# The head of a hybrid decoder step computed by halves of the channels

## What is computed

```python
def rmsnorm(x, g):
    xf = x.astype(jnp.float32)
    y = xf * lax.rsqrt(jnp.mean(xf * xf, axis=-1, keepdims=True) + EPS)
    return y.astype(x.dtype) * g

def modulate(x, g, shift, scale):
    return rmsnorm(x, g) * (1 + scale[:, None, :]) + shift[:, None, :]
...
        mod = (jax.nn.silu(c) @ ada_w[i] + ada_b[i]).reshape(c.shape[0], N_MOD, D_MODEL)
        hn = modulate(x, norm_g[i, 0], mod[:, 0], mod[:, 1])
...
            out, C1, n1, m1 = mlstm_mixer(hn, C0s[j], n0s[j], m0s[j], mlstm_w_in[j],
                                          mlstm_b_gates[j], mlstm_head_g[j], mlstm_w_out[j])
```

## Time and profile before

| what | us |
|---|---|
| median of 3 runs | 1310.14 |
| lowest and highest | 1308.98 and 1311.0 |
| the profiled execution's own time | 1309.41 |
| its span | 1307.7 |
| PE busy | 1269.4 |
| ScalarE, VectorE, GpSimd busy | 504.7, 772.1, 367.6 |

### The profile page before, as it was taken

One profiled execution on the slowest core, in us unless ns is written; L12 is line 12 of the kernel. 1 busy time (PEld: TensorE's weight loads), 2 busy tenths in 40 slices (PEclk: granted clock), 3 DMA queues, 4 the chain that ended last, 5 costly groups with the idle time before them and its releaser, 6 DMA issues.

```text
span 1307.7 us, 26354 instructions
## 1 busy us (share of the span) xinstructions
PE 1269.4 (97%) x11305; PEld 1243.4 (95%) x11305; DVE 772.1 (59%) x1296; ACT 504.7 (39%) x792; POOL 367.6 (28%) x184
## 2 busy tenths in 40 slices
PE   5799999999999999999999999999999999999996
PEld 4799999999999999999999999999999999999996
DVE  2623445667757643643659809859859743824764
ACT  3533453222532551551552322123362551642721
POOL 2434433443300041041044245435310041050050
PEclk9999999999999999999999999999999999999998
DMA  9667214754456574574553233323132242342321
GB/s 332 204 193 177 80 55 122 230 169 123 135 173 195 161 229 126 162 228 128 160 165 97 65 97 92 86 83 97 53 94 81 68 134 60 97 132 62 98 65 69
DMA packets 242526, 169.34 MB, mean 129 GB/s; under 512 B 5851, under 2 KB 217055, under 8 KB 242282
## 3 DMA queue, kind: packets, MB, share of 16 engines
q1 hardware_dynamic: 215946, 121.33, 32.4%
q10 hardware_dynamic: 26304, 46.27, 10.9%
q0 software_dynamic: 160, 0.07, 0.0%
HBM read 160.70 MB, written 6.94 MB: 128 GB/s over the span
## 4 chain that ended last, share of the span: by engine, by line
PE 80%; DVE 10%; issue 3%; DMA 3%; SPq 2%; ACT 2%; POOL 1%; POOLq 0%; DVEq 0%; ACTq 0%
PE G L1922 39%; PE G L2042 19%; PE G L1948 9%; PE G L2078 6%; PE B L2106 3%; SPq L462 1%; DVE hb L1396 1%; DMA raw<-in_mlp_w_down 1%; DVE small_s L1847 1%; DVE acc L1273 1%; DMA early<-in_ada_w 1%; PE B L1908 1%; DVE yc L1846 1%; DVE Xl L1410 1%; PE B L2290 1%
## 5 line engine op out<-in xcount | busy, mean ns | idle before, releaser
L1087 POOL TENSOR_TENSOR wl<-raw,wh 128x1024 fp32r<-128x1024 f32 x128 | 326.4, 2558 | 784.1 <-ACT wh L587 781.2
L587 ACT ACTIVATE wh<-raw 128x1024 fp32r<-128x1024 f32 x144 | 152.1, 1056 | 277.0 <-PE G L1922 147.4
L1922 PE MATMUL G<-Hh,wh 128*128 128x272 f32 x864 | 179.3, 289 | 0.0
L1922 PE MATMUL G<-Hh,wl 128*128 128x272 f32 x864 | 178.4, 288 | 0.0
L1922 PE MATMUL G<-Hl,wh 128*128 128x272 f32 x864 | 178.3, 288 | 0.0
L1922 PE MATMUL G<-Xh,wh 128*128 128x272 f32 x672 | 143.1, 294 | 1.0 <-POOL wl L1087 1.0
L1922 PE MATMUL G<-Xl,wh 128*128 128x272 f32 x672 | 138.7, 288 | 0.0
L1922 PE MATMUL G<-Xh,wl 128*128 128x272 f32 x672 | 138.3, 287 | 0.0
L1922 PEld LDWEIGHTS G<-Hh,wh 128*128 128x128 f32 x864 | 135.5, 188 | 1.0 <-issue 1.0
L1922 PEld LDWEIGHTS G<-Hl,wh 128*128 128x128 f32 x864 | 135.8, 189 | 0.0
L1922 PEld LDWEIGHTS G<-Hh,wl 128*128 128x128 f32 x864 | 135.0, 189 | 0.0
(11 more groups left out here) (385 smaller groups left out, 2732.0 us busy)
## 6 DMA issues: line engine op xcount, KB each, us to landing
raw<-in_mlp_w_up SPq DMA_DIRECT2D x64, 512.0 KB, 4.2
raw<-in_mlp_w_down SPq DMA_DIRECT2D x64, 512.0 KB, 4.4
aring<-in_ada_w ACTq DMA_DIRECT2D x60, 512.0 KB, 5.1
raw<-in_mlstm_w_in SPq DMA_DIRECT2D x24, 512.0 KB, 4.3
raw<-in_conv_w_in SPq DMA_DIRECT2D x24, 512.0 KB, 3.7
early<-in_ada_w SPq DMA_DIRECT2D x16, 512.0 KB, 12.2
free_l<-in_ada_w ACTq DMA_DIRECT2D x20, 256.0 KB, 6.8
raw<-in_mlstm_w_out SPq DMA_DIRECT2D x8, 512.0 KB, 4.7
```

Of the source, the lines that this page charges most:

```text
L587: nc.scalar.activation(wh[:, t % SLOTS], raw_of(t), ACT.Copy).then_inc(s_hi, 1)
L1087: nc.gpsimd.tensor_tensor(wl[:, t % SLOTS], raw_of(t), wh[:, t % SLOTS].bitcast(F32), ALU.subtract).then_inc(s_lo, 1)
L1922: last = mm(G[:, 2 * (g % 2) + hf, 0:HALF], w[:, s, k, :], x[:, k, hf * HALF:(hf + 1) * HALF], start=st, stop=en)
```

## The change

The head is reordered so that channel blocks 0 to 3 go all the way to operands, gates and QK products before blocks 4 to 7 are scaled.

- `ADA_ORDER` swaps the first two sections: tiles 0 to 7 are now the scale and 8 to 15 the shift. SyncE fetches tiles 0 to 3 and 8 to 11 first, then the two `raw` tiles, then 4 to 7 and 12 to 15. Some tiles lie elsewhere in SBUF.
- The products of tiles 8 to 15 go to the bank `B6`, so `ada_pair(4)` no longer waits for VectorE.
- The roots are copied from PSUM to `xr` in SBUF, and `xn` is computed from there, four blocks at a time.
- `first_mod`, `first_norm`, `first_norm_low` and `first_norm_hi` do one half (`q`) of the blocks each.
- On PE, `gates(0)` to `gates(3)`, then `ada_pair(2)` and `(3)`; then `head_pair` runs QK tiles 0 and 1 together: tile 0's blocks 0 to 3, `ada_pair(6)` and `(7)`, tile 1's blocks 0 to 3, then for each of blocks 4 to 7 tile 0, tile 1 and the gate.
- ScalarE's weight copies for tiles 2 and 3 come behind all norm operands.

```diff
-ADA_ORDER = (0, 1, 2, 4, 3, *range(5, 2 * NMOD))
+ADA_ORDER = (1, 0, 2, 4, 3, *range(5, 2 * NMOD))
+EARLY = (0, 1, 2, 3, 8, 9, 10, 11, 4, 5, 6, 7, 12, 13, 14, 15)
...
-            for a in range(2, ADA_RING):
+            for a in EARLY[2:8]:
                 ada_fetch(nc.sync, a)
             unit(T_QK, w_in, 0, order=range(RAWS))
+            for a in EARLY[8:]:
+                ada_fetch(nc.sync, a)
             for a in range(ADA_RING, ADA_RING + ADAS):
                 ada_fetch(nc.sync, a)
...
+            def first_norm_hi(q):
+
+                ks = slice(4 * q, 4 * q + 4)
+                act.wait_ge(s_sm, q + 1)
+                for k in range(4 * q, 4 * q + 4):
+                    full = dict(bias=modT[:, 0, k, 0:1], scale=gain[:, k, 0:1])
+                    nc.scalar.activation(prompt(Xh[:, k, :]), prompt(xn[:, k, :]), ACT.Identity, **full).then_inc(s_hhi, 1)
...
+                    if k % 2:
+                        if k >= 2:
+                            act.wait_ge(s_kx, X_NORM0 + k - 1)
+                        nc.scalar.activation(prompt(hb[1][:, :]), prompt(xn[:, k, :]), ACT.Identity, **full).then_inc(s_hx, 1)
+                        if q == 0:
+                            hi(k // 2)
...
-            act.wait_ge(s_au, ADA_RING)
-            norm_hi(0, 0, 0)
+            first_norm_hi(0)
+            first_norm_hi(1)
+            hi(2)
             hi(3)
...
+            def first_mod(n, q):
+
+                d, ks = ADA_ORDER[n], slice(4 * q, 4 * q + 4)
+                dve.wait_ge(s_au, 8 * q + 4 * n + 4)
+                turned = V.transpose(adaT[:, 4 * n:4 * n + 4, :].rearrange("p m s -> p (m s)"),
+                                     (B4, B6)[n][:, P * q:P * (q + 1)])
...
+            def first_norm(q):
+
+                ks, gcol = slice(4 * q, 4 * q + 4), 96 + 4 * q
+                half = samp[:, ks, :].rearrange("p k (b t) -> p k b t", t=ST)
+                first_mod(0, q)
+                chain.link(V.tensor_scalar(gain[:, ks, :], modT[:, 1, ks, :], 1.0, None, ALU.add))
+                chain.link(V.tensor_tensor(gain[:, ks, :], gain[:, ks, :],
+                                           par0[:, gcol:gcol + 4].unsqueeze(2).broadcast_to((P, 4, NSEQ)), ALU.mult))
+                chain.link(V.tensor_tensor(half, half, seq_cols(gain)[:, ks], ALU.mult))
+                first_mod(1, q)
+                V.tensor_tensor(half, half, seq_cols(modT[:, 0])[:, ks], ALU.add).then_inc(s_sm, 1)
...
+            chain.link(V.tensor_copy(halves(xr[:, :]), rstd))
+
+            def scaled_x(ks):
+                for k in ks:
+                    dve.wait_ge(s_xe, k + 1)
+                    last = V.tensor_tensor(prompt(xn[:, k, :]), prompt(xT[:, k, :]), prompt(xr[:, :]), ALU.mult)
+                chain.link(last)
...
+            scaled_x(range(4))
             dve.wait_ge(s_gs, 1)
             V.tensor_tensor(gl[:, :, :], graw[:, :, :], gh[:, :, :].bitcast(F32), ALU.subtract).then_inc(s_gs, 1)
...
+            first_norm(0)
+            first_norm_low(0)
+            scaled_x(range(4, KT))
+            first_norm(1)
+            first_norm_low(1)
...
-                if k % 4 == 0 and n:
+                if k % 4 == 0 and n >= 2:
                     pe.wait_ge(s_tr, n)
+                out = B6 if n == 1 else ada_out
...
-            for k in range(1, 8):
+            ada_pair(1)
+            pe.wait_ge(s_xse, 1)
+            for k in (4, 5):
                 ada_pair(k)
...
-            gates(0)
-            gates(1)
+            for k in range(4):
+                gates(k)
+            ada_pair(2)
+            ada_pair(3)
+
+            def head_pair(t, g, xh, xl, j, per_t, per_g, ready):
+
+                def steps(k, o):
+                    if (k, o) == (3, 0):
+                        ada_pair(6)
+                        ada_pair(7)
+                    if k >= 4 and o == 1:
+                        gates(k)
+
+                order = (*((k, o) for o in range(2) for k in range(4)), *((k, o) for k in range(4, KT) for o in range(2)))
+                pair_steps(t, g, xh, xl, HALF, order, slots_drained(g), ready, steps)
...
-            mixed(T_QK, G_QK, 2, Xh, Xl, None, post=post_k, between=lambda m: (lambda k: gates(k + 2) if m == 0 and k + 2 < KT else None))
+            mixed(T_QK, G_QK, 2, Xh, Xl, x_ready(X_NORM0), post=post_k, pair=head_pair)
```

More of the change, by code:

```diff
@@ L182, in build_program @@
         Xl = sb("Xl", [P, KT, TOK], F32R)
-        early1 = sb("early1", [P, 8, 2, QW], at=at_X)
+        early_x = [sb(f"early_x{i}", [P, 2, 2, QW], at=at_X + (8 * i + 4) * ROW) for i in range(2)]
         batch = sb("batch", [P, KT, 2, QW], at=at_X)
@@ L190, in build_program @@
         xn = sb("xn", [P, KT, TOK], at=at_h)
+        early_h = sb("early_h", [P, 3, 2, QW], at=at_h + (NJ + 1) * D * 4)
         vtok = sb("vtok", [P, NJ, H, DVA], at=at_h)
@@ L260, in build_program @@
         ktok = sb("ktok", [P, NJ, H * DK], at=at_f + 16 * ROW)
+        early_f = sb("early_f", [P, 2, QW], at=at_f + 16 * ROW)
         kam = [sb(f"kam{i}", [NS, SB, P], at=at_f + 16 * ROW + i * SB * P * 4) for i in range(2)]
@@ L318, in ada_tile @@
                 return batch[:, a % KT]
-            return aring[:, a % ADAS] if a >= ADA_RING else (early0 if a < 8 else early1)[:, a % 8]
+            if a >= ADA_RING:
+                return aring[:, a % ADAS]
+            if a % KT < 4:
+                return early0[:, a // KT * 4 + a % 4]
+            if a < KT:
+                return early_x[a // 2 % 2][:, a % 2]
+            return early_h[:, a - 12] if a < ADA_RING - 1 else early_f[:, :, :]
         def slot(g):
@@ L743, in raw_hi @@
             def raw_hi(n, k):
-                act.wait_ge(s_gn, n + 1)
+                act.wait_ge(s_gn, n)
                 act.wait_ge(s_dr, done((0, G_WOUT, G_MLP0_LAST + 8, G_COUT)[n] + k + 1))
@@ L841, in norm_hi @@
                 sh = layer * NMOD + 3 * which
-                if n == 0:
-                    samples()
                 for k in ks:
[L845 to L854, removed]
                     act.wait_ge(s_hh, KT * (n - 1) + k + 1)
@@ L1320, in norm_gain @@
                                 par0[:, gcol:gcol + KT].unsqueeze(2).broadcast_to((P, KT, NSEQ)), ALU.mult).then_inc(s_gn, 1)
[L1321 to L1333, removed]
+                dve.wait_ge(s_gn, n)
+            def first_mod(n, q):
[3 more added lines that the diff above has]
+                                     (B4, B6)[n][:, P * q:P * (q + 1)])
+                if q:
+                    turned.then_inc(s_tr, 1)
+                    dve.wait_ge(s_tr, n + 1)
+                else:
+                    chain.link(turned)
+                added = V.tensor_tensor(modT[:, d, ks, :], adaT[:, 4 * n:4 * n + 4, 0:NSEQ],
+                                        par0[:, d * KT + 4 * q:d * KT + 4 * q + 4].unsqueeze(2).broadcast_to((P, 4, NSEQ)), ALU.add)
+                if q:
+                    added.then_inc(s_mod, 1)
+                    dve.wait_ge(s_mod, n + 1)
+                else:
+                    chain.link(added)
@@ new lines, in first_norm_low @@
+            def first_norm_low(q):
+                ks = slice(4 * q, 4 * q + 4)
+                for k in range(4 * q, 4 * q + 4):
+                    if k % 2 == 0:
+                        if k >= 2:
+                            dve.wait_ge(s_kx, X_NORM0 + k - 1)
+                        chain.link(V.tensor_scalar(prompt(hb[0][:, :]), prompt(xn[:, k, :]), gain[:, k, 0:1],
+                                                   modT[:, 0, k, 0:1], ALU.mult, ALU.add))
+                    if k % 4 == 0:
+                        dve.wait_ge(s_smh, q + 1)
+                        V.tensor_tensor(samples_of(Xl)[:, ks], samp[:, ks, :].rearrange("p k (h c) -> p k h c", h=2),
+                                        samples_of(Xh)[:, ks].bitcast(F32), ALU.subtract)
+                    if k % 2:
+                        dve.wait_ge(s_hx, k // 2 + 1)
+                    dve.wait_ge(s_hhi, k + 1)
+                    V.tensor_tensor(prompt(Xl[:, k, :]), prompt(hb[k % 2][:, :]), prompt(Xh[:, k, :].bitcast(F32)),
+                                    ALU.subtract).then_inc(s_kx, 1)
@@ L1525, in _ @@
             spread_diag(0)
+            dve.wait_ge(s_root, 1)
+            dve.wait_ge(s_xse, 1)
+            chain.link(V.tensor_copy(halves(xr[:, :]), rstd))
[4 more added lines that the diff above has]
+                chain.link(last)
+            dve.wait_ge(s_xt, KT)
+            chain.link(V.tensor_tensor(samp[:, :, :].rearrange("p k (h c) -> p k h c", h=2), samples_of(xT),
+                                       sample(xr[:, :]).unsqueeze(1).broadcast_to((P, KT, 2, SH)), ALU.mult))
+            scaled_x(range(4))
             dve.wait_ge(s_gs, 1)
             V.tensor_tensor(gl[:, :, :], graw[:, :, :], gh[:, :, :].bitcast(F32), ALU.subtract).then_inc(s_gs, 1)
[L1528 to L1552, removed]
+            first_norm(0)
[3 more added lines that the diff above has]
```

(7 more changed lines are left out.)

12 lines of the change are left out of this document (7 added, 5 removed).

## The result

The changed kernel takes **1312.65 us** (median of 13 runs, 1311.63 to 1314.79), the kernel before 1310.95 in the 13 runs that go with them (1308.98 to 1311.6). The ratio is estimated from all runs and not from the two medians, which differ by 1.70 us: it is 1.002, with an interval (95%) of 1.0013 to 1.0027. The change is slower by 1.7 to 3.5 us, with the middle on the bound of 0.2%. The profiled execution of the changed kernel took 1314.08 us, in the upper part of its runs.

A forecast was written before the change was run, and what follows sets the result against it. PE bounds the kernel, so head delays reach the end whole. Tile 2 starting later (+1.3) and lost clock (+1.6) give +2.9 us on the median 1310.14: 1313.0, eight-in-ten range 1309.7 to 1316.0.

The forecast's parts named there:

- First half, earlier: VectorE in the head: first half's samples ready at 28.3 instead of 37.64, so the first four blocks run 9.3 us earlier.
- The copied roots: VectorE's `xn` for blocks 4 to 7: held by GpSimd's second subtraction to about 40.0 instead of 37.9; nothing charged.
- PE between the halves: PE from gates 2 and 3, at half clock, to the shift's second half: tile 0 starts at 39.7, products done at 44.6.
- Second half: Blocks 4 to 7: first low part ends at 47.7; last gate, tile 0 and tile 1 end together at 56.6.
- What is late next: Tile 2 waits for ScalarE's store of tile 0, 7.54 us after the last gate: PE stands 6.5 us, start +1.3.
- The clock: PE after standing 6.5 us: about 3.2 us at half clock, +1.6 us, bounds 0 and 3.4.
- rival A: No change: clock doesn't fall in the new wait, or PE between halves runs at full clock; 1308.7 to 1311.5, chance 0.18.
- Other queues: SyncE's `raw` fetch for tile 4 lands at 62.7, ScalarE wants it at 62.5: 0.2 us, left in the range.
- Rival C: Faster: tile 0's slot freed in time, so the head is worth its 5.3 us; 1304.8, chance 0.08.

The follow-up runs named there:

- e1: Changed kernel with ScalarE storing QK tiles 0 and 1 before it waits for the gate rows: 1305.97 us, ratio 0.9968 to the kernel before.
- e2: Kernel before the change with ScalarE storing QK tiles 0 and 1 ahead of the gate rows: 1311.26 us, ratio 1.0007.
- e7: Changed kernel with ScalarE's weight copy of tile 1, and so GpSimd's second subtraction, behind VectorE's second scaling: 1313.51 us, ratio 1.0024 to the kernel before.
- e3: Changed kernel without the pair, PE doing all of tile 0 with gates 4 to 7, then tile 1: 1310.17 us, ratio 0.9998 to the kernel before.
- e4: Changed kernel with 50 extra matmuls, results unused, in PE's wait ahead of tile 2: 1314.2 us, ratio 1.003 to the kernel before.
- e5: Changed kernel again, unaltered, on a second chip: 1313.59 us, ratio 1.0026 to the kernel before.
- e6: Changed kernel with 30 extra matmuls, results unused, in PE's wait ahead of tile 2: 1313.02 us, ratio 1.0021 to the kernel before.

## Why the prediction was right, point by point

The forecast was 1313.0 us, and 1312.65 was measured. Its cause, the wait for tile 0's store, is shown by `e1`, by `e2` as its control, and by the trace. That the size agrees so closely is in part luck, as the last points say. In the profiled execution the modulation products began at 24.23 instead of 22.57, ahead of any matmul that the change moves. So 1.66 is to be added to the predicted times; the sum with it stands in brackets.

- *First half, earlier.* The samples of the first half were to be ready at 28.3 (30.0); measured 30.03.
- *The copied roots.* The copy took 0.72 us against 0.73, `xn` was held for 4.66 - 2.50 = 2.16 against 2.1, and it cost nothing, as charged; `e7` confirms both. The Trainium skill names the condition in "GPSIMD Engine Reference", section "Key points": GpSimd shares its SBUF interfaces with VectorE and contends with operations that have two SBUF inputs. The traces agree, with 4.66 us here and 2.30 in `e7`.
- *PE between the halves.* Tile 0's blocks were to start at 39.7 (41.4); measured 41.28, with gates 2 and 3 at half clock as assumed. In the traces of `e3`, `e4` and `e7` those gates had the full clock, so the assumption holds for some executions only. The products of the shift's second half were to be done at 44.6 (46.3); measured 46.43.
- *Second half.* Its first low part was to end at 47.7 (49.4); measured 49.49, and PE did not wait. The last gate was to end at 56.6 (58.3); measured 58.81, since the 96 matmuls took 12.4 us instead of 12.0.
- *What is late next.* The chain from the last gate to the store was 7.54 and measured 7.47; the wait was to be 6.5 and measured 6.65. Tile 2 starts 3.56 later than before: 1.66 from ahead of the change, and 1.9 where the sum had +1.3.
- *The clock.* 1.6, measured 1.64 in the profiled execution. The clock was lost in all three traces with the wait of 6.65 us (the changed kernel's, `e5` and `e7`), so this term is borne out there. In the profiled execution the sum is 2.9 + 1.66 = 4.56 us, and 4.67 was measured against 1309.41. Even there two small differences cancel: tile 2's start and the clock make 3.56 + 1.64 = 5.20, and what follows took 0.5 us less than before.
- *The median.* Here luck comes in. The medians differ by 1.70 us and the ratio gives 2.6, less than those 4.67. The 13 runs fall into eight of 1311.63 to 1312.65 (mean granted clock 0.993 or 0.994) and five of 1313.90 to 1314.79 (0.991), with medians 1312.24 and 1314.08: 1.3 and 3.1 us above the 1310.95 of before. The profiled execution is of the second kind. What the eight were spared isn't shown, since none of them was traced. It could be the clock's loss in the wait, or the slow stretch between the halves, which the sum took as given. The trace of `e7` speaks for the second: its mean clock is 0.994, and it lost the clock in the wait all the same but not between the halves. That is the second condition of rival A, so the median has something of the forecast and something of A.
- *Other queues.* There was no wait for the fetch of tile 4: its copy started at 64.73, right behind the logarithm.

Open is the 1.66. In three traces of kernels with the old head the products began at 22.18 to 23.25 (median 22.57), in seven with the new one at 22.63 to 24.51 (24.16). The two overlap, but part of the later start may belong to the change, and the sum has no term for it. It isn't the clock, which is 1.00 in both traces from 16 to 24 us.

Rival C named the right place and nearly the right price: it needed the chain from last gate to store to be shorter than 3.7 us. `e1`, which takes the gates out of it, gained 4.2 us on the kernel before by the ratio, against C's 5.3.

## What to carry to other kernels

When a change brings a producer forward, list every wait that the old matmuls covered, with its length; the next of them becomes the bound, and its length less what is still over it is the price. An engine runs its queue in order: put whatever frees a PSUM slot ahead of work that waits for another result, and try that together with the head's change, since neither alone gave a gain here (1.002 and 1.0007, together 0.9968). A filler that keeps PE busy in a wait is no substitute for taking the wait away.

## What the runs showed of the hardware

After 6.65 us of standing the full clock was lost in all three traces that have this wait. After the shorter gaps between the halves (5.2 and 1.4 us ahead of gates 0 and 2) it was not the same in every execution: gate 2 ran at 1.2 GHz in four traces (the changed kernel's, `e1`, `e5`, `e6`) and at 2.4 GHz in three (`e3`, `e4`, `e7`), with the same program on PE up to there. After a wait of 2.83 us the fall came 1.3 us into the work (`e6`), so a full clock at the first matmul behind a wait does not yet mean that nothing is lost.

The mean granted clock of an execution doesn't say where the loss lay: 0.994 in `e7` and 0.991 in the changed kernel's trace go with the same loss behind the wait.

GpSimd's hold does not depend on how small VectorE's operation is: 128x36 with two inputs in SBUF took 2.30 us instead of 0.20 (`e7`), and ended within 0.1 us of GpSimd's end at 43.45. What counts is how much of GpSimd's operation is left when VectorE begins. Nor is it confined to two tensor inputs. In the kernel before, `hb` (line 1548, 128x512, one tensor in SBUF with a scale and a bias per partition) took 2.62 us instead of 0.54 beside the second subtraction:

```profile
44.76 2.62 DVE L1548 TENSOR_SCALAR hb<-xn,gain,modT 128x512 f32<-128x512 f32 x1
```
